# Two fused transformer blocks on one core: the level masks of the RWKV inverse made by GpSimd in place of VectorE

## The chip, the core and the metric
One NeuronCore of a Trainium2 chip runs the whole program, one launch for one sequence of 512 tokens. The metric is the device time of that launch in microseconds (us), lower is better. Engines are named as in the profile: PE (TensorE matmul), PEld (its weight load), DVE (VectorE), ACT (ScalarE), POOL (GpSimd), SP (SyncE, here only the queue that loads weights).

## What is computed
The reference runs two transformer blocks on x of 512 x 1024, float32. The first mixes a dilated window attention with an RWKV-7 layer, gates and merges both, projects, and adds a squared-ReLU feed-forward. The second mixes a pooling branch with a windowed attention and ends in a gated feed-forward. The change lies in the RWKV-7 layer, whose recurrence, cut to what matters, is for each of 16 heads of width 64:

```
def step(state, inp):
    r_t, w_t, k_t, v_t, kk_t, a_t = inp
    sa = einsum('bhij,bhj->bhi', state, -kk_t)
    state = state * w_t + sa * (kk_t * a_t) + v_t * k_t
    y_t = einsum('bhij,bhj->bhi', state, r_t)
    return state, y_t
```

The kernel computes it in four chunks of 128 tokens. Within a chunk the 128 dependent values of sa are found at once: with a strictly triangular matrix A (the gram of the decayed keys against each other), sa comes out of the inverse of a unit triangular matrix made of A. That inverse is built by doubling: blocks of 2, 4, 8, up to 128 tokens, seven levels. At each level the part of A that links the two halves of each block is taken out by multiplying A with a 0/1 mask of that level, and two rounds of matmuls bring the inverse from one block size to the next.

## The kernel before
**Weights.** Every product with a weight is made of three float32r matmuls (high times high, high times low, low times high; lines 572 to 574 of the trace). Weights come in units of 128 x 2048 into a ring of three slots. SP loads a unit (w_raw), ACT copies its high part (w_hi, line 1215), and the low part w_lo = w_raw - w_hi is written over w_raw. POOL does this in a loop over all 138 units (line 563), except for the units from DVE_LO0 to DVE_LO1 - 1, which belong to the RWKV stage: their low parts are made by DVE (weights_behind, line 1880).

**The RWKV stage.** Heads are handled in 8 pairs. For each pair the arrays are 128 x 512 (128 partitions, 4 chunks of 128), and there is one of each per head of the pair (index h = 0, 1). The stage is a software pipeline over steps p from -2 to 7: in step p, pair a = p is in its last phase (the recurrence over chunks, the norm), pair b = p + 1 is in the inverse, pair c = p + 2 is in its first phase (decay, keys, bonus). Every engine has its own written-out order of the parts of a step, and all waits are on counting semaphores. PE also has slots in each step that it fills with pieces of the projections of later pairs (side_half, three 512-column matmuls each): these are the matmuls of lines 572 to 574 in this stage. Such a half can begin only when the half before has been taken out of its PSUM bank (shift_half on DVE, lines 1816 and 1817, whose other input gate_tile comes from ACT, line 1309).

**The inverse of pair b, engine by engine.** PE makes the gram (inverse_grams, line 944). DVE copies its strict triangle of both heads into GA, named gram_inv (line 1963), and then makes level 0's masked gram Mb, named level (line 1957), one instruction per head. PE turns it (level_x, line 956, level 0). DVE's level_first then makes TT = Mb + I (line 1970, named tinv_t) and Tb = x + I (line 1972, named tinv) for each head, and after both makes the masks of level 1. From level 1 on: PE's level_x multiplies Mb with Tb (line 956), DVE adds the identity (level_x, line 1979, named xinv), PE's level_t makes both products (lines 964 and 966), ACT copies them back to TT and Tb (lines 1431 and 1432). At the end a refinement (lines 973, 1984, 980, 1989) gives the inverse that pair a's recurrence uses (line 1004). The masks of levels 2 to 6 stand at places of their own in DVE's step, each right before or some operations before the next level's matmuls need them. There is one Mb per head, so a mask can be written only once the matmuls of the level before have read the last one.

**The start of a step** is a chain through engines: PE's bonus sum (line 915), DVE's bonus (1947), tinv_full (1989) and kb (1952, 1953), PE's gram (944), DVE's gram_inv (1963), the masks of level 0 (1957), PE's level_x (956). Meanwhile PE has the sigmoid inputs of pair c (882) and the first solve of pair a (1004) to do.

Of the kernel before, what the change touches and what calls it, by code (L numbers as in the profile page):

```python
# [12 lines left out]
ALU = mybir.AluOpType  # L13
AX = mybir.AxisListType

P = 128
T = 512
NT = T // P
# [17 lines left out]
PAIRS = 8  # L36
# [5 lines left out]
LEVELS = (2, 4, 8, 16, 32, 64, 128)  # L42
# [91 lines left out]
CC = {}  # L134
# [64 lines left out]
def build(nc, x, wpack, lora_wa, lora_g, params, rel_bias, post_gains, sink, ctab, btab, icount, out):  # L199
# [7 lines left out]
    with ExitStack() as ctx:  # L207
# [9 lines left out]
        def fixed(name, shape, dt=F32):  # L217
            return place(name, shape, dt)[0]
# [12 lines left out]
        def sem(name):  # L231
            return ctx.enter_context(nc.semaphore(name))
# [13 lines left out]
        C = fixed("consts", [P, N_EARLY_CCOLS])  # L246
# [61 lines left out]
        GA = [r(f"gram_inv{h}", [P, NT, P]) for h in range(2)]  # L308
        Mb = [r(f"level{h}", [P, NT, P], F32R) for h in range(2)]
# [79 lines left out]
        rs = {n: sem(n) for n in (  # L389
            "z_full", "sig_ready", "zg_full", "g_ready", "sq_ready", "ss_full", "nrm_ready", "rn_ready", "rnx_ready", "rb_full",  # L390
            "kk_ready", "rk_ready", "bonus_full", "bon_ready", "csm_ready", "exps_ready", "xexp_ready", "ra_ready",
            "kb1_ready", "kb_ready", "tok_full", "tok_ready", "agram_full", "gram_full", "gram_taken", "m_ready",
            "x_full", "x1_ready", "tt_full", "t_ready", "t2_ready", "s_ready", "rhs_full", "rhs_ready", "sa_full",
            "sa_ready", "s_full", "y_full", "yraw_ready", "mu_full", "ysq_ready", "var_full", "std_ready",
            "rv_ready", "rvx_ready", "rvb_full", "rvm_ready", "u_full", "e_ready", "c_full", "tf_ready")}

# [33 lines left out]
        DVE_LO0, DVE_LO1 = UNIT0["gate1_first"], UNIT0["rwkvb"] + 1  # L430
# [35 lines left out]
        def f32(ap):  # L466
            return ap.bitcast(F32)
# [14 lines left out]
        for hp in range(2):  # L482
            for qt in range(NT):
                mats, vals, off = [], [[], []], 0
                for g in range(N_GROUPS):
                    nb = min(2, qt + 1) if g == 0 else qt + 1
                    k0 = (qt + 1 - nb) * P
                    for e in range(2):
                        h = g * 4 + 2 * hp + e
                        rows = slice(HD * e, HD * e + HD)  # L490
                        b, c0 = (3 + 2 * g - 2 + e, 0) if g else (2, 256 * e)
# [16 lines left out]
        for j in range(Q_HEADS2 // 2):  # L508
            for qt in range(NT):
# [4 lines left out]
                n = (hi - lo) * P  # L514
                pairs2.append(dict(
                    n=n, j=j, rows=rows, bias=AD[:, x0:x0 + n], out=O2[:, j, qt * P:(qt + 1) * P],
# [37 lines left out]
        @block.gpsimd  # L554
        def _(pool):


            for n in range(N_UNITS):
                if DVE_LO0 <= n < DVE_LO1:
                    continue  # L560
                slot = n % RING
                pool.wait_ge(hi_ready, n + 1)
                nc.gpsimd.tensor_tensor(Wl[:, slot, :], raw[:, slot, :], f32(Wh[:, slot, :]),  # L563
                                        ALU.subtract).then_inc(lo_ready, 1)
# [1170 lines left out]
        def _(dve):  # L1735
            order = Order(dve, dve_order)
            v = nc.vector
# [89 lines left out]
            for i, it in enumerate(pairs1):  # L1827
                st, n = 16 + 8 * (i % 2), it["n"]
# [4 lines left out]
                for m in it["mats"]:  # L1833
                    ins = v.scalar_tensor_tensor(LG[:, m["e"], m["off"]:m["off"] + m["n"]], m["dst"], HD ** -0.5, m["bias"],
                                                 ALU.mult, ALU.add)
# [20 lines left out]
            def cast4(ap):  # L1856

                return ap.unsqueeze(1).to_broadcast([P, NT, P])

            nl = len(LEVELS)  # L1860
# [3 lines left out]
            def lmask(lv):  # L1864
                return cast4(C[:, CC["levels"] + lv * P:CC["levels"] + (lv + 1) * P])

            def w(name, per, pair, k):
                dve.wait_ge(rs[name], per * pair + k)

            def inc(ins, name):  # L1870
                ins.then_inc(rs[name], 1)
# [15 lines left out]
            def shift_half(n):  # L1887
                if n is not None and HALVES[n][0] == "rkv":
                    kind, pair, part = HALVES[n]
                    shift(N_SHIFTED[n], RKV[:, pair % 2, part, :], 0, GT, 8 * part + pair)  # L1890
# [61 lines left out]
                inc(v.tensor_tensor(KB[:, 1, :], Ab[:], X2[:], ALU.mult), "kb1_ready")  # L1952
                inc(v.tensor_tensor(KB[:, 0, :], kk_, X2[:], ALU.mult), "kb_ready")

            def level_mask(b, lv):
                for h in range(2):
                    inc(v.tensor_tensor(Mb[h][:], GA[h][:], lmask(lv), ALU.mult), "m_ready")  # L1957

            def inverse_grams(b):
                w("agram_full", 1, b, 1)  # L1960
                v.memset(stat[:, 40:41], 0.0)
                for h in range(2):
                    ins = v.copy_predicated(GA[h][:], mask[:, P:2 * P].unsqueeze(1).to_broadcast([P, NT, P]), b3(4 + h))
                order(ins)
                level_mask(b, 0)

            def level_first(b):
                for h in range(2):
                    w("m_ready", 2 * nl, b, h + 1)
                    v.tensor_tensor(TT[h][:], f32(Mb[h][:]), cast4(ident), ALU.add)  # L1970
                    w("x_full", 2 * nl, b, h + 1)
                    inc(v.tensor_tensor(Tb[h][:], b3(4 + h), cast4(ident), ALU.add), "t2_ready")
                w("t2_ready", 2, b, 2)
                level_mask(b, 1)

            def level_x(b, lv):
                for h in range(2):
# [13 lines left out]
            def solved(a, t):  # L1991
                w("sa_full", NT, a, t + 1)
                inc(v.tensor_copy(SA[:], ps[:, 3, P:2 * P]), "sa_ready")
# [37 lines left out]
            def step(p):  # L2031

                a, b, c = p, p + 1, p + 2
                has_a, has_b, has_c = 0 <= a, 0 <= b < PAIRS, c < PAIRS
                first, middle, _ = STEP_HALVES[p]
                last = STEP_HALVES[p - 1][2] if p > -2 else None
                if has_b:
                    inverse_grams(b)
                shift_half(last)
                if has_a:  # L2040
                    solved(a, 0)
                if has_b:
                    level_first(b)
                if has_a:
                    state(a, 0)
                weights_behind(last)
                if has_c:
                    key_squares(c)
                if has_b:
                    level_x(b, 1)  # L2050
                if has_a:
                    solved(a, 1)
                if has_b:
                    level_mask(b, 2)
                if has_a:
                    state(a, 1)
                if has_c:
                    decay_sums(c)
                    key_scale(c)
                if has_b:  # L2060
                    level_x(b, 2)
                if has_a:
                    solved(a, 2)
                if has_b:
                    level_mask(b, 3)
                if has_a:
                    state(a, 2)
                shift_half(first)
                if has_c:
                    key_root(c)  # L2070
                if has_b:
                    level_x(b, 3)
                if has_a:
                    solved(a, 3)
                if has_c:
                    bonus_terms(c)
                    decay_args(c)
                if has_b:
                    level_mask(b, 4)
                if has_c:  # L2080
                    key_norm(c)
                    rates(c)
                weights_behind(first)
                if has_b:
                    level_x(b, 4)
                if has_a:
                    centred(a)
                if has_b:
                    level_mask(b, 5)
                    level_x(b, 5)  # L2090
                if has_c:
                    queries(c)
                if has_b:
                    level_mask(b, 6)
                shift_half(middle)
                if has_b:
                    grams(b, 0)
                if has_a:
                    norm_root(a)
                if has_b:  # L2100
                    level_x(b, 6)
                    grams(b, 1)
                weights_behind(middle, 0)
                if has_a:
                    normed(a)
                if has_b:
                    grams(b, 2)
                weights_behind(middle, 1)
                if has_b:
                    refine_e(b)  # L2110
                    grams(b, 3)
                if has_c:
                    bonus(c)
                if has_b:
                    refine_t(b)
                if has_c:
                    keys(c)
# [94 lines left out]
            for i, it in enumerate(pairs2):  # L2212
                st, n = 16 + 8 * (i % 2), it["n"]
# [4 lines left out]
                for h in range(2):  # L2218
                    ins = v.scalar_tensor_tensor(LG[:, h, 1:n + 1], it["bias"], it["slopes"][h], bank(4 + h, n),
                                                 ALU.mult, ALU.add)  # L2220
# [28 lines left out]
            for g in range(FF2_GROUPS):  # L2249
                d = USE0["ffn2"] + 2 * g  # L2250
                dve.wait_ge(hid_raw, FF1_GROUPS + g + 1)
                h = HID[:, 2 * g:2 * g + 2, :]
# [91 lines left out]
```

## Time and profile before

| | us |
|---|---|
| median of 3 runs | 1986.84 (1982.43 to 1988.65) |
| the profiled execution, its own time | 1984.22 |
| its span in the profile | 1982.4 |
| PE busy | 1875.3 (95%) |
| DVE busy | 881.5 (44%) |
| ACT busy | 760.0 (38%) |
| POOL busy | 514.0 (26%) |

The stage that the change touches runs from about 313 us (the first mask) to about 813 us. In it DVE is busy for three quarters of the time and POOL not at all. The page is an average over stages with different limits, so the busy shares above say little of this stage; it has to be read from windows of its own.

### The profile page before, as it was taken

Reading aid. Unit: us, or ns where it says so; the run is one execution under the profiler, and the core shown is the slowest. Engines: PE = TensorE matmul, PEld = TensorE weight load, DVE = VectorE, ACT = ScalarE, POOL = GpSimd, SP = SyncE. Lnnn points to the kernel's source line nnn. Section 1 sums busy time; section 2 is a strip of 40 time slices with the busy share of each in tenths; the row PEclk is TensorE's granted clock in tenths of the full one; section 3 lists DMA queues with packets and bytes.
Section 4 is the critical chain, followed back from the end, with each engine's and each line's share of the span. In section 5 each row is a group of like instructions: output and inputs, shape, how many; then the busy total and the mean of one; then the engine's idle time right before and its main releaser. Section 6 shows DMA issues by size and latency. Waiting matters only on the chain.

```text
span 1982.4 us, 23689 instructions
## 1 busy us (share of the span) xinstructions
PE 1875.3 (95%) x10148; PEld 1549.8 (78%) x10148; DVE 881.5 (44%) x1321; ACT 760.0 (38%) x1099; POOL 514.0 (26%) x115
## 2 busy tenths in 40 slices
PE   6999878999999999899899999989999999999998
PEld 5887656878878888688788888877776788888886
DVE  2015436687778776443301344351774341013333
ACT  5226534445544553423422222252564242222222
POOL 2431200000000000034243444423223424343432
PEclk8999988899999999999999999999999999999999
DMA  4711122000100000243223232322112223232221
GB/s 152 249 65 64 59 70 61 25 25 22 44 27 25 22 22 32 89 150 113 105 97 103 89 106 85 106 89 91 64 64 85 85 96 106 86 106 90 101 101 70
DMA packets 54508, 160.74 MB, mean 81 GB/s; under 512 B 3295, under 2 KB 30303, under 8 KB 39684
## 3 DMA queue, kind: packets, MB, share of 16 engines
q1 hardware_dynamic: 42476, 135.40, 19.8%
q10 hardware_dynamic: 11928, 23.83, 3.5%
q8 instruction: 80, 1.31, 0.3%
q14 instruction: 24, 0.20, 0.0%
HBM read 152.63 MB, written 10.25 MB: 82 GB/s over the span
## 4 chain that ended last, share of the span: by engine, by line
PE 83%; ACT 7%; DVE 7%; issue 1%; DMA 1%; POOL 0%; ACTq 0%; DVEq 0%
PE ps L572 23%; PE ps L573 22%; PE ps L574 22%; PE ps L956 2%; PE ps L966 2%; PE ps L964 2%; ACT w_hi L1215 1%; PE ps L1040 1%; PE ps L688 1%; ACT tinv_t L1431 1%; PE ps L1004 1%; PE ps L973 1%; DVE level L1957 1%; DVE x_res L1768 1%; PE ps L666 1%
## 5 line engine op out<-in xcount | busy, mean ns | idle before, releaser
L563 POOL TENSOR_TENSOR w_lo<-w_raw,w_hi 128x2048 fp32r<-128x2048 f32 x111 | 513.8, 4629 | 1438.3 <-ACT w_hi L1215 1438.3
L572 PE MATMUL ps<-ht_hi,w_hi 128*128 128x512 f32 (+1 forms) x1304 | 529.3, 406 | 22.3 <-DVE ht_lo L1754 9.9
L574 PE MATMUL ps<-ht_hi,w_lo 128*128 128x512 f32 (+1 forms) x1304 | 502.3, 385 | 0.0
L573 PE MATMUL ps<-ht_lo,w_hi 128*128 128x512 f32 (+1 forms) x1304 | 502.3, 385 | 0.0
L1215 ACT ACTIVATE w_hi<-w_raw 128x2048 fp32r<-128x2048 f32 x126 | 240.9, 1914 | 489.0 <-PE ps L574 430.6
L572 PEld LDWEIGHTS ps<-ht_hi,w_hi 128*128 128x128 f32 x1304 | 250.8, 192 | 84.5 <-issue 32.7
L574 PEld LDWEIGHTS ps<-ht_hi,w_lo 128*128 128x128 f32 x1304 | 250.4, 192 | 49.3
L573 PEld LDWEIGHTS ps<-ht_lo,w_hi 128*128 128x128 f32 x1304 | 251.3, 193 | 39.5 <-issue 2.2
L2161 DVE TENSOR_TENSOR hid_lo<-hidden,hid_hi 128x1024 fp32r<-128x1024 f32 x27 | 129.3, 4788 | 149.1 <-ACT hid_hi L1580 149.1
L572 PE MATMUL ps<-w_hi,hid_hi 128*128 128x512 f32 x432 | 168.1, 389 | 0.0
L574 PE MATMUL ps<-w_hi,hid_lo 128*128 128x512 f32 x432 | 168.1, 389 | 0.0
L573 PE MATMUL ps<-w_lo,hid_hi 128*128 128x512 f32 x432 | 168.1, 389 | 0.0
L574 PEld LDWEIGHTS ps<-w_hi,hid_lo 128*128 128x128 f32 x432 | 81.1, 188 | 16.9
L572 PEld LDWEIGHTS ps<-w_hi,hid_hi 128*128 128x128 f32 x432 | 81.1, 188 | 16.8
L573 PEld LDWEIGHTS ps<-w_lo,hid_hi 128*128 128x128 f32 x432 | 81.1, 188 | 16.7
L572 PE MATMUL ps<-w_hi,ht_hi 128*128 128x512 f32 (+2 forms) x256 | 86.6, 338 | 2.1 <-POOL w_lo L563 2.1
L1431 ACT ACTIVATE tinv_t<-ps 128x512 fp32r<-128x512 f32 x96 | 57.7, 601 | 78.2 <-PE ps L966 78.2
L573 PE MATMUL ps<-w_lo,ht_hi 128*128 128x512 f32 (+2 forms) x256 | 86.5, 338 | 0.0
L574 PE MATMUL ps<-w_hi,ht_lo 128*128 128x512 f32 (+2 forms) x256 | 86.5, 338 | 0.0
L2170 DVE TENSOR_TENSOR hidden<-ps,gate_act 128x1024 f32<-128x1024 f32 x16 | 19.6, 1225 | 134.1 <-ACT gate_act L1619 134.1
L1957 DVE TENSOR_TENSOR level<-gram_inv,consts 128x512 fp32r<-128x512 f32 x112 | 72.1, 685 | 0.6
L1979 DVE TENSOR_TENSOR xinv<-ps,consts 128x512 fp32r<-128x512 f32 x96 | 61.3, 678 | 19.0 <-PE ps L956 18.8
(290 smaller groups left out, 2595.9 us busy)
## 6 DMA issues: line engine op xcount, KB each, us to landing
w_raw<-in_wpack SPq DMA_DIRECT2D x114, 1024.0 KB, 4.8
w_raw<-in_wpack SPq DMA_DIRECT2D x24, 512.0 KB, 5.2
bias_skewed_dram<-bias_rows_dram ACTq DMA_DIRECT2D x1, 3840.0 KB, 22.9
toe<-bias_skewed_dram ACTq DMA_DIRECT2D x1, 3072.0 KB, 13.2
x_res<-in_x SPq DMA_DIRECT2D x4, 512.0 KB, 5.6
merged<-gate_dram ACTq DMA_DIRECT2D x1, 2048.0 KB, 11.1
gate<-gate_dram ACTq DMA_DIRECT2D x1, 2048.0 KB, 13.3
x_res<-in_x ACTq DMA_DIRECT2D x1, 2048.0 KB, 8.8
```

Of the source, the lines that this page charges most:

```text
L563: nc.gpsimd.tensor_tensor(Wl[:, slot, :], raw[:, slot, :], f32(Wh[:, slot, :]), ALU.subtract).then_inc(lo_ready, 1)
L572: mm(dst, wh, ah, start=first, stop=False)
L573: mm(dst, wh, al, start=False, stop=False)
L574: return mm(dst, wl, ah, start=False, stop=last)
L956: last = mm(ps[:, 4 + h, tok(t)], Mb[h][:, t, :], Tb[h][:, t, :] if lv else identR[:], start=True, stop=True)
L964: mm(ps[:, 6 + h, tok(t)], Xb[h][:, t, :], TT[h][:, t, :], start=True, stop=True)
L966: last = mm(ps[:, 4 + h, tok(t)], TT[h][:, t, :], Xb[h][:, t, :], start=True, stop=True)
L1215: actf(Wh[:, n % RING, :], raw[:, n % RING, :], ACT.Copy).then_inc(hi_ready, 1)
L1431: actf(TT[h][:].rearrange("p a b -> p (a b)"), bank(6 + h), ACT.Copy)
L1957: inc(v.tensor_tensor(Mb[h][:], GA[h][:], lmask(lv), ALU.mult), "m_ready")
L1979: inc(v.tensor_tensor(Xb[h][:], b3(4 + h), cast4(ident), ALU.add), "x1_ready")
L2161: v.tensor_tensor(HIl[:, 2 * g:2 * g + 2, :], HID[:, 2 * g:2 * g + 2, :], f32(HIh[:, g % RING, :, :]), ALU.subtract).then_inc(hid_lo, 1)
```

## The change
The 112 mask instructions (8 pairs, 7 levels, 2 heads) leave DVE and are issued by POOL. POOL does them in one block of its program, between the low part of the last unit before the RWKV stage and that of the first unit after DVE's own. DVE's copy of the gram now signals ga_ready in place of the wait that ordered it before the masks. POOL waits for ga_ready at level 0 and, at level 1, for t2_ready of the same head (DVE has then read Mb for TT). For every mask but the first two it also waits for x_full of the level before and the same head, so that PE has read Mb. Nothing is changed in PE's and ACT's programs, nor in DVE's except for the masks, the order wait and DVE's own wait on t2_ready. The instruction is the same in shape: 128 x 512, the gram times a mask of 128 columns repeated over the four chunks.

```diff
         @block.gpsimd
         def _(pool):
+            nl = len(LEVELS)
+
+            def level_mask(b, lv, h):
+
+                if lv == 0:
+                    pool.wait_ge(rs["ga_ready"], b + 1)
+                if lv == 1:
+                    pool.wait_ge(rs["t2_ready"], 2 * b + h + 1)
+                if b or lv:
+                    pool.wait_ge(rs["x_full"], 2 * (nl * b + lv - 1) + h + 1)
+                cols = C[:, CC["levels"] + lv * P:CC["levels"] + (lv + 1) * P].unsqueeze(1).to_broadcast([P, NT, P])
+                nc.gpsimd.tensor_tensor(Mb[h][:], GA[h][:], cols, ALU.mult).then_inc(rs["m_ready"], 1)
+
             for n in range(N_UNITS):
                 if DVE_LO0 <= n < DVE_LO1:
+                    if n == DVE_LO0:
+                        for b in range(PAIRS):
+                            for lv in range(nl):
+                                for h in range(2):
+                                    level_mask(b, lv, h)
                     continue
...
-            def level_mask(b, lv):
-                for h in range(2):
-                    inc(v.tensor_tensor(Mb[h][:], GA[h][:], lmask(lv), ALU.mult), "m_ready")
-
             def inverse_grams(b):
...
-                order(ins)
-                level_mask(b, 0)
+                inc(ins, "ga_ready")
 
             def level_first(b):
...
                     inc(v.tensor_tensor(Tb[h][:], b3(4 + h), cast4(ident), ALU.add), "t2_ready")
-                w("t2_ready", 2, b, 2)
-                level_mask(b, 1)
...
-                if has_b:
-                    level_mask(b, 2)
```

The calls for levels 3 to 6 leave DVE's step in the same way.

## Rows read from the trace of the kernel before

**Rows 1.** The page: busy time, and the chain that ended last, by engine.
```profile
PE 1875.3 (95%) x10148; PEld 1549.8 (78%) x10148; DVE 881.5 (44%) x1321; ACT 760.0 (38%) x1099; POOL 514.0 (26%) x115
...
PE 83%; ACT 7%; DVE 7%; issue 1%; DMA 1%; POOL 0%; ACTq 0%; DVEq 0%
```

**Rows 2.** Windows, step p = 1, and the sum of all eight: each engine's busy us.
```profile
435.40:498.20 62.80, 61.04 (x431) 51.02 (x431) 48.45 (x93) 31.51 (x52) 0.00 (x0) 1.00 0.08 21
...
sum 499.40, PE 476.87 PEld 402.89 DVE 372.40 ACT 243.25 POOL 0.00; mean PE 59.61 PEld 50.36 DVE 46.55 ACT 30.41 POOL 0.00
```

**Rows 3.** Waits of PE, 300 to 810 us: total us, times, longest.
```profile
PE ps L964 <- DVE xinv L1979: 5.0, 3, 3.2
...
PE ps L572 <- DVE rkv L1817: 4.8, 12, 0.6
PE ps L956 <- DVE level L1957: 3.9, 5, 1.3
PE ps L944 <- DVE kb L1952: 2.6, 2, 1.3
```

**Rows 4.** Groups of DVE by form, 300 to 810 us: masks and DVE's own low parts.
```profile
L1957 DVE TENSOR_TENSOR level<-gram_inv,consts 128x512 fp32r<-128x512 f32 x112 | 72.1, 685 | 0.6
...
L1880 DVE TENSOR_TENSOR w_lo<-w_raw,w_hi 128x2048 fp32r<-128x2048 f32 x8 | 18.3, 2285 | 0.1
```

**Rows 5.** Groups and waits of POOL over the whole span.
```profile
L563 POOL TENSOR_TENSOR w_lo<-w_raw,w_hi 128x2048 fp32r<-128x2048 f32 x111 | 513.8, 4629 | 1438.3 <-ACT w_hi L1215 1438.3
L2334 POOL MEMSET const-bfloat16-1.0<- 128x1 bf16 x1 | 0.1, 102 | 0.0
...
POOL w_lo L563 <- ACT w_hi L1215: 1438.3, 109, 594.6
```

**Rows 6.** Timelines of POOL and DVE at one hid_lo (start, us); DVE's group.
```profile
1100.49 4.61 POOL L563 TENSOR_TENSOR w_lo<-w_raw,w_hi 128x2048 fp32r<-128x2048 f32 x1 [6.28 <-ACT w_hi L1215]
...
1101.39 4.79 DVE L2161 TENSOR_TENSOR hid_lo<-hidden,hid_hi 128x1024 fp32r<-128x1024 f32 x1 [1.52 <-ACT hid_hi L1580]
...
L1880 DVE TENSOR_TENSOR w_lo<-w_raw,w_hi 128x1024 fp32r<-128x1024 f32 x8 | 9.6, 1213 | 3.5 <-ACT w_hi L1215 3.5
```

**Rows 7.** Timeline of DVE at the start of step p = 1.
```profile
436.07 0.71 DVE L1963 COPY_PREDICATED gram_inv<-consts,ps 128x512 f32<-128x512 int32 x1
436.82 1.29 DVE L1957 TENSOR_TENSOR level<-gram_inv,consts 128x512 fp32r<-128x512 f32 x2
438.03 0.74 DVE L1816 SCALAR_TENSOR_TENSOR rkv<-ps,one_less_mu,gate_tile 128x511 f32<-128x511 f32 x1
...
439.14 0.68 DVE L1970 TENSOR_TENSOR tinv_t<-level,consts 128x512 fp32r<-128x512 f32 x1
...
441.66 1.29 DVE L1957 TENSOR_TENSOR level<-gram_inv,consts 128x512 fp32r<-128x512 f32 x2
```

**Rows 8.** Timeline of PE in the same stretch.
```profile
437.57 1.26 PE L956 MATMUL ps<-ident_r,level 128*128 128x128 f32 x8 [0.73 <-DVE level L1957]
...
442.40 1.26 PE L956 MATMUL ps<-tinv,level 128*128 128x128 f32 x8
```

**Rows 9.** Step p = -1: DVE's low part behind the masks, and PE's wait for xinv.
```profile
318.52 2.29 DVE L1880 TENSOR_TENSOR w_lo<-w_raw,w_hi 128x2048 fp32r<-128x2048 f32 x1
...
322.58 0.66 PE L964 MATMUL ps<-tinv_t,xinv 128*128 128x128 f32 x4 [1.47 <-DVE xinv L1979]
```

**Rows 10.** Later in step p = 1: DVE's xinv of levels 4 and 5, and PE.
```profile
470.05 1.28 DVE L1979 TENSOR_TENSOR xinv<-ps,consts 128x512 fp32r<-128x512 f32 x2
...
474.96 1.29 DVE L1979 TENSOR_TENSOR xinv<-ps,consts 128x512 fp32r<-128x512 f32 x2 [0.93 <-PE ps L956]
...
480.32 0.50 PE L572 MATMUL ps<-ht_hi,w_hi 128*128 128x512 f32 x1 [0.31 <-DVE rkv L1817]
```

**Rows 11.** Windows at the starts of steps p = 1 and p = 2, with PE's granted clock.
```profile
436.00:442.30 6.30, 5.45 (x34) 4.12 (x33) 6.20 (x13) 1.97 (x2) 0.00 (x0) 1.00 0.00 0
499.00:505.30 6.30, 5.40 (x29) 4.24 (x28) 6.20 (x12) 2.42 (x4) 0.00 (x0) 0.73 0.31 130
```

More of the change, by code:

```diff
@@ L392, in build @@
             "kb1_ready", "kb_ready", "tok_full", "tok_ready", "agram_full", "gram_full", "gram_taken", "m_ready",
-            "x_full", "x1_ready", "tt_full", "t_ready", "t2_ready", "s_ready", "rhs_full", "rhs_ready", "sa_full",
+            "ga_ready", "x_full", "x1_ready", "tt_full", "t_ready", "t2_ready", "s_ready", "rhs_full", "rhs_ready", "sa_full",
             "sa_ready", "s_full", "y_full", "yraw_ready", "mu_full", "ysq_ready", "var_full", "std_ready",
@@ L2063, in step @@
                     solved(a, 2)
-                if has_b:
-                    level_mask(b, 3)
                 if has_a:
@@ L2077, in step @@
                     decay_args(c)
-                if has_b:
-                    level_mask(b, 4)
                 if has_c:
@@ L2088, in step @@
                 if has_b:
-                    level_mask(b, 5)
                     level_x(b, 5)
@@ L2092, in step @@
                     queries(c)
-                if has_b:
-                    level_mask(b, 6)
                 shift_half(middle)
```

## The prediction
> **What bounds the kernel now.** The page first: PE is busy for 95% of the span, and the chain that ended last runs through PE for 83% of it and through DVE for 7% [rows 1]. That says only that PE is the engine to watch. The change touches one stage, so the second view is windows cut at the starts of the steps. A full step takes 63 us and PE is busy for 61 of them; over the eight steps it is busy for 476.9 of 499.4 us [rows 2]. DVE, with 48 of 63 us, is well used but not the bound, and POOL does nothing. So 22.5 us of PE's idle time is all that shorter queues can win back, unless PE's clock also changes. The third view, PE's waits, shows which part of the idle time is DVE's: xinv 5.0, rkv 4.8, the masks themselves 3.9, kb 2.6, together 16.3 us [rows 3]. The question is which of these shrink and which grow.
>
> **The price of one mask.** On DVE it takes 685 ns, and 112 of them are 72.1 us of DVE's busy time, 9 us of each step [rows 4]. The trace has no POOL instruction of this size. Its only worker takes 4629 ns for 2048 columns, and its smallest instruction 102 ns [rows 5]. Below: all of it in proportion, 4629 / 4 = 1157 ns. Above: if POOL's time per column were no more than DVE's, (2285 - 1213) / 1024 = 1.05 ns [rows 4, 6], the fixed part would be 4629 - 2144 = 2485 ns and a mask would take 3.0 us. I take 1.2 us, next to the lower end, because a fixed part of over 2 us does not go with an instruction of 102 ns. The two heads' masks follow each other, 2.4 us, where DVE needs 1.29.
>
> What the pages would make of it: the Trainium skill (GPSIMD Engine Reference, 3.1 Elementwise) measures such an operation at 1.96 times VectorE's time. By that a mask is 1.34 us (an estimate from that page), 0.14 more than I take, and with two masks at eight step starts the sum would be 2.2 us higher. No row shows this size.
>
> **POOL and DVE in each other's way.** DVE's hid_lo, 128 x 1024 with both inputs in SBUF, starts 0.90 us after a POOL low part has started and takes 4.79 us; the same kind and size takes 1.21 us while POOL rests. POOL ends at 1105.10 and hid_lo at 1106.18, 1.08 us behind [rows 6]. So DVE did not run slower, it stood until POOL was through. Taking this as it reads, a DVE instruction with two inputs in SBUF stands up to 1.2 us behind a POOL mask, and one whose other input is in PSUM (xinv, rkv, tinv) is taken as free. The Trainium skill has this as a rule (SBUF — State Buffer, Who interferes with whom): such a VectorE instruction and a GpSimd one that reads SBUF exclude each other for their whole length, whichever comes first. By that rule POOL can also stand behind DVE; the trace agrees for DVE behind POOL, with the 4.79 us. Without any such exclusion the first-step term below (+1.7) would fall away.
>
> **Part 1: level 0, at the start of each step.** Before: DVE's second gram_inv ends at 436.78, the masks run from 436.82 to 438.11, PE's level_x starts at 437.57 after an idle 0.73, does head 0 and head 1 without a break and ends at 438.83 [rows 7, 8]. After: POOL starts at about 436.86, head 0 is ready at 438.06 and head 1 at 439.26. PE starts at 438.1 (0.6 later), stands again between the heads, and ends head 1 at 439.26 + 0.6 = 439.9, 1.1 us later than before. What hides it? Nothing: PE takes its work in order, and the side matmul behind it waits. DVE's rkv shift comes 1.2 us earlier, since the masks no longer stand before it, but it only removes a wait that would have been over anyway. PE's end of level 0 thus moves by 1.1 us in each of eight steps: **+8.8 us**. It is +8.0 at 1157 ns and some +37 at 3.0 us (3.6 later for head 1, plus the 1.1).
>
> **Part 2: level 1.** DVE's level_first now waits in DVE's queue for m_ready from POOL. Behind it stand pair a's state, the low part w_lo, pair c's key squares and xinv. TT of head 0 reads Mb and the identity, both in SBUF, so it stands until head 1's mask ends at 439.26, where it started at 439.14 before [rows 7]. Hardly later, then. Its four operations end at about 441.7 as before. POOL's masks of level 1 start behind TT of head 1 (440.5 to 441.1): head 0 at 442.3, head 1 at 443.5. Before, they were there at 442.34 and 442.95. PE comes to level_x of level 1 at 442.40 [rows 8], now at 443.5: on time. So **0** in a full step, between 0 and +0.6 (if PE comes no later than before). In the first step PE has no pair a to work on. Head 1's mask of level 1 would end near 320.2, and w_lo (2.29 us, two SBUF inputs) starts behind it, where it started at 318.52; xinv and PE's level_t, which already waited 1.47 us [rows 9], follow 1.7 us later: **+1.7**. If w_lo gets in first, the mask comes 2.3 us later still; that is the upper end, +4.
>
> **Part 3: levels 2 to 6.** POOL may start a mask as soon as PE's level_x of the level before is done; PE needs it one xinv, eight matmul groups and two ACT copies later, 4.9 us at the least in step p = 1, from xinv of level 4 to xinv of level 5 [rows 10]. Two masks take 2.4. They are off the path, at 0, and held behind a w_lo of 2.29 us they would still be there in time, at 4.7. DVE loses ten masks at 0.6 us of spacing, but it does not get all of it: the masks now run right beside xinv, and the next DVE operation with two SBUF inputs (decay sums, bonus terms, squares, queries) stands for up to 1.1 us behind the second. Some half comes through. The PE wait it can shorten is that of 0.31 us for the rkv shift that stands behind level 6's masks [rows 10]; the rest of the rkv waits hang on ACT's gate_tile. 0.31 us in six full steps: **-1.9 us**. Ends: 0, and -12.4, which is all of the waits for xinv, rkv and kb in rows 3.
>
> **Part 4: PE's clock.** At the start of step p = 2 the granted clock is 0.73 in a window of 6.3 us, so PE spent part of it at 1.2 in place of 2.4 GHz; at the start of step p = 1, with the same busy time, it stayed at 1.00 [rows 11]. Both had short stops just before. Cost of one such drop: 0.27 x 6.3 = 1.7 us. The same windows at the seven starts from p = 0 on show a drop at five (0.52 to 0.88) and none at p = 1 and 4. With a stop that grows from 0.7 to over 1.3 us, and a second between the heads, one of these two falls, I take it: **+1.7 us**, between 0 and +7 (both, and longer ones elsewhere).
>
> **Part 5: POOL's queue.** The masks stand before the low part of the first unit behind the stage. POOL's longest wait is 594.6 us [rows 5]; that gap holds the stage, so 112 x 1.2 = 134 us fit in. DVE's last mask ended near 795 us, the stage near 813. No DMA is issued by POOL or DVE, and SP's loads wait for PE alone. **0.** If the cover were gone, a low part would come one mask late, 1.2 us, once.
>
> **Sum:** 8.8 + 0 + 1.7 - 1.9 + 1.7 + 0 = +10.3 us. On the profiled execution's own 1984.22 us this is 1994.5. That execution is 2.6 us below the median shown, 1986.84; a median of new runs should stand by the median, so the forecast is **1997 us**, 0.52% above. About 0.3% (6 us) is what a measurement of this kernel can tell from no change.
>
> **The rivals.**
> - *The delay is absorbed* (0.26). The 1.1 us at level 0 is partly paid by time that PE would idle later in the step (1.8 us per full step, rows 2), and DVE's lighter queue takes more of it away. For: the rkv waits, 12 of them. Against: what PE waits for later was itself started by PE, and moves with it. Half of part 1 gone and the clock unchanged: 4.4 + 1.7 - 1.9 = +4.2, 1991 us.
> - *Faster* (0.12). The mechanism is DVE's queue: with 9 us less in each step every DVE result comes before PE asks. The waits for xinv, rkv and kb go (-12.4), and four of the five step starts with a clock drop keep the full clock (-1.7 each, -7). Level 0 costs 8.8 as above. Net -10.6: 1976 us. It decides where DVE's delay, and not PE's or ACT's own work, is what starts a step; against it speaks that PE had to wait for kb, DVE's last work of a step, only twice [rows 3].
> - *The exclusion makes masks late everywhere* (0.10). DVE has long two-input operations between levels; if POOL loses its turn to them at each level, PE waits 0.6 us at levels 1 to 6 in eight steps, 29 us, and the sum is +39: 2026 us; half of the levels give 2011. Against it: the 4.9 us between levels.
> - *The change does not do what it says* is no case here: m_ready is only counted by POOL's masks.
>
> **How the numbers follow.** The forecast has 0.52, with its own range +6 to +17, 1993 to 2004 (parts 2 and 4 at their ends, a mask of 1.3 us). The range runs from 1985 to 2010: it leaves out most of the faster case and the far half of the late-mask case. Faster by over 0.3%: 0.12. Within: the absorbed case and the forecast's low edge, 0.28. Slower: 0.60.
>
> **What would show it.** POOL would show 112 masks of 1.15 to 1.35 us in the stage. DVE's busy time there falls by less than 72 us, because tinv_t, scans, kb or squares that stand behind POOL are shown longer than 0.7 us. PE's wait for level at level 0 would rise from 3.9 us to about 12, and a full step from 63 to 64 us. More windows at step starts would show a clock under 1. The forecast is wrong if the step stays at 63 us or less, if PE's waits for level don't grow, or if they appear at levels 2 to 6 too.

## The result and the profile after

The changed kernel takes 2005.37 us in the median of 4 runs (2003.70 to 2006.06) against 1987.31 us before: a ratio of 1.0094, 95% interval 1.0076 to 1.0112, so 18 us or 0.9% slower. The forecast was slower, 1997 us, with 1985 to 2010 as the range. The profiled execution has a span of 2003.4 us, 21.0 more than that of the kernel before.

The page of the changed kernel, the lines that answer to [rows 1] and the new group on POOL:

```profile
PE 1892.7 (94%) x10148; PEld 1564.1 (78%) x10148; DVE 834.7 (42%) x1209; ACT 760.3 (38%) x1099; POOL 643.8 (32%) x227
...
PE 81%; issue 6%; ACT 6%; DVE 5%; POOL 1%; DMA 1%; ACTq 0%; DVEq 0%; POOLq 0%
...
L569 POOL TENSOR_TENSOR level<-gram_inv,consts 128x512 fp32r<-128x512 f32 x112 | 130.1, 1182 | 418.0 <-DVE gram_inv L1977 206.4
```

DVE lost 72.1 us of masks but is only 46.8 us less busy: 25 us came back as other instructions that are shown longer. PE has the same 10148 matmuls and is 17.4 us longer busy with them. That is work at a lower clock (windows below), and it is the first hint that PE's standing is only part of the loss.

PE's waits in the changed kernel, from 300 to 840 us, to be read against [rows 3] (L974 is level_x, L982 level_t, L590 the side matmul):

```profile
PE ps L974 <- POOL level L569: 11.2, 13, 2.4
...
PE ps L982 <- DVE xinv L1990: 5.4, 7, 3.3
PE ps L962 <- DVE kb L1970: 2.6, 2, 1.3
PE ps L590 <- DVE rkv L1835: 2.6, 5, 0.6
```

The wait for the masks grew from 3.9 to 11.2 us, that for rkv fell from 4.8 to 2.6. Windows cut at the first gram copy of each step tell what each cost. First the kernel before, steps p = -1, 0 and 5, then the changed one; PE's busy time is the fourth number, the granted clock the third from the end:

```profile
312.20:369.90 57.70, 49.59 (x309) 42.16 (x308) 40.06 (x75) 26.55 (x44) 0.00 (x0) 0.90 0.14 44
369.90:435.40 65.50, 64.53 (x431) 53.77 (x431) 50.38 (x95) 31.07 (x52) 0.00 (x0) 0.93 0.07 19
...
690.00:753.50 63.50, 59.73 (x406) 50.34 (x404) 47.69 (x91) 30.17 (x50) 0.00 (x0) 0.92 0.06 17
```

```profile
312.50:377.00 64.50, 54.95 (x309) 46.34 (x309) 34.69 (x59) 26.69 (x44) 18.45 (x14) 0.81 0.13 39
377.00:443.50 66.50, 65.32 (x431) 54.03 (x431) 44.17 (x82) 31.07 (x52) 15.55 (x14) 0.93 0.07 19
443.50:508.20 64.70, 62.18 (x431) 52.12 (x430) 43.01 (x79) 31.52 (x52) 15.84 (x14) 0.97 0.08 22
...
703.90:771.70 67.80, 62.84 (x406) 53.27 (x404) 41.94 (x77) 30.28 (x50) 16.99 (x14) 0.87 0.06 16
```

Two sums over the seven steps from p = -1 to p = 5 divide the loss. **Idle** is length less PE's busy time. **Clock loss** is (1 - granted clock) x length. The seven steps took 441.3 us before and 459.2 after, 17.9 more. Idle went from 20.4 to 26.2, clock loss from 19.3 to 33.6. Length is idle plus busy time, so of the 17.9 us, 5.8 are PE standing, a third, and 12.1 are PE busy for longer with the same matmuls. The clock loss tells why: it grew by 14.3, PE working at 1.2 in place of 2.4 GHz for a while after it stood. (It is not the 12.1 exactly, since it also counts the slow clock while PE stands, and the clock is given with two digits: 0.01 of a step is 0.6 us.) The first step alone grew by 6.8 us, of which 1.4 are idle, and p = 5 by 4.3. The other 3.1 of the 21.0 us between the two profiles lie behind the stage.

The timelines at the start of step p = 1 show a hand-over. First POOL, then DVE and PE:

```profile
444.89 2.14 POOL L569 TENSOR_TENSOR level<-gram_inv,consts 128x512 fp32r<-128x512 f32 x2 [23.07 <-DVE gram_inv L1977]
448.26 2.52 POOL L569 TENSOR_TENSOR level<-gram_inv,consts 128x512 fp32r<-128x512 f32 x2 [1.23 <-DVE tinv L1985]
```

```profile
446.02 1.56 DVE L1983 TENSOR_TENSOR tinv_t<-level,consts 128x512 fp32r<-128x512 f32 x1
...
446.04 0.66 PE L974 MATMUL ps<-ident_r,level 128*128 128x128 f32 x4 [1.17 <-POOL level L569]
447.09 0.66 PE L974 MATMUL ps<-ident_r,level 128*128 128x128 f32 x4 [0.39 <-POOL level L569]
...
448.01 0.63 PE L591 MATMUL ps<-ht_lo,w_hi 128*128 128x512 f32 x1
```

A mask takes 1.07 us. PE stands 1.17 and 0.39 us where it stood 0.73, and the 512-column matmul behind takes 0.63 us, not 0.40: the clock has fallen, in a step that kept it before [rows 11]. The matmul of the same place in the kernel before:

```profile
439.29 0.40 PE L573 MATMUL ps<-ht_lo,w_hi 128*128 128x512 f32 x1
```

DVE's tinv_t needs 1.56 us for 0.68 because it stands until POOL's second mask ends at 447.03.

### The profile page after: what moved, and what is told of

It reads as the page before. It is cut to its first block, busy times and chain, and to the rows that moved or that the text cites. A ratio compares the mean times of both kernels' runs of the same rounds, so it can differ in the third digit from the quotient of the medians.

```text
span 2003.4 us, 23719 instructions
## 1 busy us (share of the span) xinstructions
PE 1892.7 (94%) x10148; PEld 1564.1 (78%) x10148; DVE 834.7 (42%) x1209; ACT 760.3 (38%) x1099; POOL 643.8 (32%) x227
## 4 chain that ended last, share of the span: by engine, by line
PE 81%; issue 6%; ACT 6%; DVE 5%; POOL 1%; DMA 1%; ACTq 0%; DVEq 0%; POOLq 0%
PE ps L590 22%; PE ps L592 21%; PE ps L591 21%; PE ps L982 2%; PE ps L974 2%; PE ps L984 2%; ACT w_hi L1233 1%; POOL level L569 1%; PE ps L706 1%; PE ps L900 1%; DVE x_res L1786 1%; PE ps L684 1%; PE ps L1048 1%; PE ps L1022 1%; PE ps L727 1%
## 5 line engine op out<-in xcount | busy, mean ns | idle before, releaser
L590 PE MATMUL ps<-ht_hi,w_hi 128*128 128x512 f32 (+1 forms) x1304 | 531.9, 408 | 18.0 <-DVE ht_lo L1772 9.0
L590 PEld LDWEIGHTS ps<-ht_hi,w_hi 128*128 128x128 f32 x1304 | 252.4, 194 | 80.0 <-issue 30.2
L569 POOL TENSOR_TENSOR level<-gram_inv,consts 128x512 fp32r<-128x512 f32 x112 | 130.1, 1182 | 418.0 <-DVE gram_inv L1977 206.4
L590 PE MATMUL ps<-w_hi,hid_hi 128*128 128x512 f32 x432 | 168.1, 389 | 0.0
L590 PEld LDWEIGHTS ps<-w_hi,hid_hi 128*128 128x128 f32 x432 | 81.1, 188 | 16.9
L1449 ACT ACTIVATE tinv_t<-ps 128x512 fp32r<-128x512 f32 x96 | 57.7, 601 | 83.0 <-PE ps L984 83.0
L590 PE MATMUL ps<-w_hi,ht_hi 128*128 128x512 f32 (+2 forms) x256 | 86.6, 338 | 2.1 <-POOL w_lo L581 2.1
```

The costliest lines, as they stand in the source:

```text
L569: nc.gpsimd.tensor_tensor(Mb[h][:], GA[h][:], cols, ALU.mult).then_inc(rs["m_ready"], 1)
L590: mm(dst, wh, ah, start=first, stop=False)
L1449: actf(TT[h][:].rearrange("p a b -> p (a b)"), bank(6 + h), ACT.Copy)
```

## The experiments

All of them are variations of the two kernels, each timed beside the kernel before on the same chip. Two theories stood at first. A: the loss comes from the hand-overs at levels 0 and 1. B: it comes from POOL and DVE excluding each other in the upper levels.

**Which levels.** A function decides who makes a mask, and each engine has a counter of its own:

```diff
+def on_pool(b, lv):
+    return lv >= 2                           # e1_high_pool
+    return lv < 2                            # e2_low_pool
+    return not (b == 0 and lv == 1)          # e3_first_dve
```

e1_high_pool. 

> Levels 2 to 6 on POOL, levels 0 and 1 back on DVE. Theory A (the loss comes from the two hand-overs to POOL at the start of each step: PE stands 1 us longer there, and its clock falls behind that): nearly all of the +18 us goes, 1984 to 1992 us; PE's idle time in the stage within 2 us of before (23.1). Theory B (POOL and DVE exclude each other, and DVE's long two-input operations stand behind the masks of levels 2 to 6): half or more of the loss stays, 1996 us or more.

Measured: 1998.1 us, ratio 1.0061 (1.0043 to 1.0080).

e2_low_pool. 

> Levels 0 and 1 on POOL, levels 2 to 6 back on DVE. Theory A: the loss is as in the full change or larger, because DVE has its 10 masks back: 2003 to 2010 us. Theory B: less than half of it, 1989 to 1996 us.

Measured: 1997.5 us, ratio 1.0060 (1.0040 to 1.0081).

Neither theory stands alone. Each half costs about 12 us by itself, and together they cost 18, so the two are not simply added. The trace of e1_high_pool shows what the upper levels do, in step p = 2. DVE, POOL, PE:

```profile
512.76 2.28 DVE L1914 TENSOR_TENSOR w_lo<-w_raw,w_hi 128x2048 fp32r<-128x2048 f32 x1
514.96 1.32 DVE L1928 TENSOR_SCALAR kk<-rkv,params_sb 128x512 f32<-128x512 f32 x1
516.31 1.46 DVE L1929 TENSOR_TENSOR work_x<-kk 128x512 f32<-128x512 f32 x1
517.70 1.27 DVE L2019 TENSOR_TENSOR xinv<-ps,consts 128x512 fp32r<-128x512 f32 x2
```

```profile
512.78 4.44 POOL L583 TENSOR_TENSOR level<-gram_inv,consts 128x512 fp32r<-128x512 f32 x2 [28.41 <-PE ps L990]
...
518.43 0.66 PE L998 MATMUL ps<-tinv_t,xinv 128*128 128x128 f32 x4 [1.84 <-DVE xinv L2019]
```

The masks of level 2 are released as soon as PE's level_x of level 1 is done, while DVE has the low part and the key squares ahead of xinv. POOL's first mask stands behind w_lo, then kk stands behind that mask (1.32 for 0.48), then work_x behind the second (1.46 for 0.69). xinv comes 1.6 us later, and PE stands 1.84 us for it. Nobody needed those masks yet. They were not late but early. In the first step the same thing makes PE stand 3.07 us for xinv, where it stood 1.47.

e3_first_dve. 

> The full change, but the two masks of level 1 of pair 0 are made by DVE, so that they no longer stand behind DVE's low part. Theory A with the sizes of the trace: the first step loses its wait of 2.44 us and the slow clock behind it, and becomes 4 to 5 us shorter: 2000 to 2002 us. If the first step's 6.8 us come from somewhere else (the clock alone, or xinv), 2004 to 2006 us.

Measured: 1999.5 us, ratio 1.0069 (1.0047 to 1.0090). The first step fell from 64.5 to 61.6 us, by 2.9 and not by 4 to 5, and the wait of 2.44 for the mask is gone; PE now stands 3.08 us for xinv there, behind level 2's early masks. All seven steps together are as long as in the change (458.9 and 459.2 us), because p = 4 and 5 are longer in this profile, and the intervals of the two ratios overlap. That the whole kernel gained by this edit is not shown.

**The clock.** In e4_filler PE works while it waits, in f1_before_filler too, with (2, 0) in place of (4, 1):

```diff
             def level_x(b, lv):
                 for h in range(2):
+                    if lv == 0:
+                        for _ in range((4, 1)[h]):
+                            mm(bank(6), identR[:], HTh[:, 0, :], start=True, stop=True)
```

e4_filler. 

> The full change, with PE made to work while it waits at level 0: four spare 512-column matmuls ahead of head 0's wait and one ahead of head 1's, results unused. If the clock is most of the loss (14 of 21 us by the windows), the drops at the step starts go and the time falls to 1991 to 1997 us, with a granted clock near 1 at the step starts. If the drops come anyhow, or the standing itself is the loss, 2003 to 2010 us.

Measured: 1999.1 us, ratio 1.0074 (1.0055 to 1.0093), less gain than expected. The interval overlaps with that of the full change (1.0076 to 1.0112), so the times alone don't show a gain. The windows are plainer. Step p = 1, changed kernel and then e4_filler:

```profile
444.00:450.30 6.30, 4.74 (x24) 3.75 (x25) 5.56 (x11) 1.97 (x2) 4.18 (x4) 0.79 0.00 1
```

```profile
444.60:450.90 6.30, 6.01 (x37) 4.39 (x37) 6.11 (x12) 1.97 (x2) 4.16 (x4) 1.00 0.00 1
```

The clock stays at 1.00, and over the seven steps the clock loss falls from 33.6 to 15.9 us and the steps by 10 us. With the same masks, the same hand-overs and only the standing filled, the drop does not come: the standing is what brings it. It does not bring it each time: in step p = 3 of e2_low_pool PE stands the same 1.17 and 0.39 us, and the clock of the step is 1.00.

f1_before_filler. 

> The kernel before, with two spare 512-column matmuls of PE ahead of head 0's wait at level 0 (results unused). In the kernel before, the windows put 22.8 us of lost time in the stage on the clock, part of it behind the starts of steps. If PE's stops at level 0 bring those drops, they go: 1976 to 1983 us, clock loss down by 4 to 10 us. If other stops bring them (ACT's rhs, kb), no change: 1984 to 1992 us.

Measured: 1984.5 us, ratio 0.9993 (0.9982 to 1.0004): no difference. In the profile the seven steps fell by 2.7 us, clock loss from 19.3 to 13.5, which the whole time does not show.

**POOL beside DVE, and nothing else.** f2_extra_pool is the kernel before, with POOL instructions whose result nobody uses (the spare row is written again later, and ACT waits for the last of them before that):

```diff
+            def extra_mask(b, lv, h):
+                pool.wait_ge(rs["x_full"], 2 * (nl * b + lv - 1) + h + 1)
...
+                nc.gpsimd.tensor_tensor(spare, cols, cols, ALU.mult).then_inc(rs["extra_made"], 1)
```

> The kernel before with all its own masks on DVE, and beside them 80 POOL instructions of a mask's size (levels 2 to 6, both inputs from SBUF, result unused), each released when the change would release it. Nothing waits for them on the path. If POOL and DVE exclude each other and this is what costs in the upper levels, the time rises by 8 us or more, 1994 to 2005 us, with xinv waits of PE in the steps whose low part stands before xinv. If the exclusion is harmless, 1984 to 1990 us.

Measured: 1995.9 us, ratio 1.0047 (1.0026 to 1.0068). 80 instructions that no engine waits for on the path cost 9 us; PE's waits for xinv rose from 5.0 to 12.0:

```profile
PE ps L979 <- DVE xinv L1996: 12.0, 10, 3.3
```

The profiled execution, 2003.7 us in span, was the longest of its five, so only the ratio is read as the cost. All masks that are used are DVE's here, as before, so neither a late mask nor a hand-over can be the reason: POOL's work beside DVE's costs time by itself, as theory B says.

**A later start.** The masks of levels 2 to 6 wait for DVE's xinv as well:

```diff
+                if lv > 1:
+                    pool.wait_ge(rs["x1_ready"], 2 * (nl - 1) * b + 2 * (lv - 2) + h + 1)
```

f3_high_late (levels 2 to 6). 

> Levels 2 to 6 on POOL as in e1_high_pool, but each mask also waits until DVE's xinv of the level before and the same head is done. Then no mask can stand in front of the operations that DVE has to get through before xinv. If the early start of the masks is the cause in e1_high_pool (waits of 3.07 and 1.84 us for xinv), they shrink to those of before and the time is 1983 to 1990 us. If the masks come too late now, PE waits for level at levels 2 to 6: 1993 us or more.

Measured: 1987.0 us, ratio 0.9994 (0.9982 to 1.0007). One wait more on POOL takes away all of the 12 us of e1_high_pool. In the first step xinv again starts behind operations of their usual length; the scan behind it pays now (2.80 for 1.36), where nobody waits:

```profile
320.66 0.69 DVE L1931 TENSOR_TENSOR work_x<-kk 128x512 f32<-128x512 f32 x1
321.27 1.28 DVE L2021 TENSOR_TENSOR xinv<-ps,consts 128x512 fp32r<-128x512 f32 x2
322.47 2.80 DVE L1936 TENSOR_TENSOR_SCAN cum_decay<-consts,sig_w 128x128 f32<-128x128 f32 x4
...
322.11 2.25 POOL L585 TENSOR_TENSOR level<-gram_inv,consts 128x512 fp32r<-128x512 f32 x2 [59.15 <-DVE xinv L2021]
```

f4_all_late (all levels). 

> The full change with the same later start of the masks of levels 2 to 6. What is left is the hand-over at levels 0 and 1: 1995 to 2000 us, as in e2_low_pool. If the two parts are not separate, 2002 us or more.

Measured: 1994.8 us, ratio 1.0047 (1.0030 to 1.0064). The full change with this wait loses half as much; the rest goes with levels 0 and 1. Of the 11.0 us between the spans of the two profiles, 5.1 lie in the seven steps, so how the gain comes about is seen only in part.

**Together.** g1 is f3 with f1's filler; g2 has more filler in pair 0's level_t, 3 matmuls at level 1 and 7 at level 3; g3 and g4 put the low levels back on POOL.

g1_high_late_filler. 

> Levels 2 to 6 on POOL with the later start (as f3_high_late), and the two spare matmuls of f1_before_filler at level 0. If what DVE gains in room and what the filler saves of the clock (5.8 us by the windows of f1_before_filler) add up, 1980 to 1984 us, clear of before. If PE's own work is the bound and both only shift its stops, 1984 to 1989 us.

Measured: 1984.2 us, ratio 0.9991 (0.9982 to 1.0000). Hardly more than nothing.

g2_more_filler. 

> The same, and in the first step of the inverse also 3 and 7 spare matmuls ahead of PE's waits for xinv at levels 1 and 3 (1.47 and 3.25 us before). If the slow clock behind these two stops goes, 3 to 5 us below g1_high_late_filler. If the filler takes PE's time from real work, the same or slower than it.

Measured: 1980.2 us, ratio 0.9971 (0.9961 to 0.9981). It beats both kernels, by 0.3% and 1.2%. The first step takes 54.0 us for 57.7, at a clock of 0.99 for 0.90, though PE does ten matmuls more in it than in g1:

```profile
313.10:367.10 54.00, 48.27 (x321) 39.47 (x321) 37.31 (x63) 26.35 (x44) 11.27 (x10) 0.99 0.15 47
```

The gain over g1 is filler alone. The kernel before has the same two waits (1.47 and 3.25 us), so it might gain by the filler too; that was not tried. Nothing here shows that POOL's masks have a part in the gain.

g3_all_late_filler. 

> All masks on POOL except level 1 of pair 0, with the later start at levels 2 to 6 and the filler of e4_filler (4 and 1) at level 0. The three causes found so far (early masks of the upper levels, pair 0's level 1 behind the low part, the clock at the step starts) are then all treated, and what is left is the hand-over itself, some 1.0 us of PE standing or of filler at eight starts: 1987 to 1993 us. If something else is in the full change's loss, 1996 us or more.

Measured: 1996.3 us, ratio 1.0056 (1.0038 to 1.0074), above the 1987 to 1993 us expected: treating the three causes was not enough. Its seven steps take 445.5 us, 4.2 over before, where the time is 10 over. Inside, step p = 2 takes 69.6 us, with this stop and a slow clock behind it:

```profile
507.18 0.66 PE L995 MATMUL ps<-tinv,level 128*128 128x128 f32 x4 [1.35 <-POOL level L585]
```

The same stop in p = 0 and p = 4 (1.35 and 1.34 us) leaves the clock at 1.00.

g4_not_one. 

> As g3_all_late_filler, with level 1 of every pair on DVE (levels 0 and 2 to 6 on POOL, later start, filler 4 and 1 at level 0). In g3_all_late_filler PE still stood 1.35 us for level 1's mask in steps p = 2 and 4, where DVE's low part follows level_first, and its clock fell behind one of them. If level 1 is what was left, those waits go, steps 2 and 4 take 63 to 64 us, and the time is 1984 to 1989 us. If level 0's hand-over is what was left, 1991 us or more.

Measured: 1992.9 us, ratio 1.0046 (1.0029 to 1.0064). The stop at level 1 is gone and p = 2 and 4 take 63.3 us each, as the one theory had it, yet the time is on the other's side. What is left sits in two steps: the first (60.9 us, PE again waits 1.46 for xinv, clock loss 9.1) and p = 5 (67.0, a new wait of 1.22 for xinv, clock loss 6.7). In all other steps of this profile level 0 on POOL costs nothing once PE's standing is filled. The times say less: the ratio is 1.0046, and the profiled execution was the shortest of the five.

The seven steps in numbers, us, worked out from each profile as above:

| kernel | length | PE idle | clock loss | ratio of times |
|---|---|---|---|---|
| before | 441.3 | 20.4 | 19.3 | 1 |
| the change | 459.2 | 26.2 | 33.6 | 1.0094 |
| e1_high_pool | 452.3 | 25.9 | 24.3 | 1.0061 |
| e2_low_pool | 451.7 | 26.5 | 25.7 | 1.0060 |
| e3_first_dve | 458.9 | 29.4 | 27.5 | 1.0069 |
| e4_filler | 449.1 | 21.7 | 15.9 | 1.0074 |
| f1_before_filler | 438.7 | 18.3 | 13.5 | 0.9993 |
| f2_extra_pool (longest of its runs) | 462.2 | 27.1 | 35.0 | 1.0047 |
| f3_high_late | 442.0 | 19.5 | 20.7 | 0.9994 |
| f4_all_late | 454.1 | 25.6 | 29.5 | 1.0047 |
| g1_high_late_filler | 438.5 | 17.5 | 14.6 | 0.9991 |
| g2_more_filler | 434.6 | 15.7 | 8.8 | 0.9971 |
| g3_all_late_filler | 445.5 | 20.8 | 13.2 | 1.0056 |
| g4_not_one | 445.2 | 17.5 | 19.1 | 1.0046 |

A profile is one execution, and its clock drops differ from the next one's; the ratios are the verdict, the columns say where. What comes behind the stage took 1167 to 1176 us in these profiles, without an order that follows the edits, so a profile's span can't settle a difference of a few us. One thing stays open. The three kernels with level 0 on POOL and the filler of 4 and 1 (e4, g3, g4) lose 9 to 15 us by their ratios, 5 to 7 us more than their seven steps show. So filling PE's standing did not win back the loss of the low levels in the whole time, and the runs don't show why.

Idle and clock loss also stand in for each other. In step p = 2 PE waits 1.38 us for a mask of level 1 in e2_low_pool, whose clock stays at 1.00, and not at all in the change. There PE works at the slow clock and comes to the matmuls of level 1 only 9.0 us behind the first gram copy, not 7.5, and by then both masks are made. The step takes 64.8 us in the one and 65.4 in the other. First e2_low_pool, then the change:

```profile
515.69 0.66 PE L990 MATMUL ps<-tinv,level 128*128 128x128 f32 x4 [1.38 <-POOL level L583]
```

```profile
517.22 1.00 PE L974 MATMUL ps<-tinv,level 128*128 128x128 f32 x8
```

## Why the prediction was right, and where its terms were not

**The price of a mask** was taken as 1.2 us with 1157 ns as the lower end. It is 1.07 (half of the 2.14 of two), below that end: a POOL instruction whose second input repeats 128 columns is not priced by the plain one in proportion. The estimate worked out from the Trainium skill (GPSIMD Engine Reference, 3.1 Elementwise), 1.34 us, is further off still: POOL's time is 1.56 times VectorE's 0.685 here, and not 1.96 times.

**Part 1, level 0: +8.8.** Right in kind, and too large. PE's head 1 ends 2.94 us behind the gram copies in step p = 1 (447.75 less 444.81) where it ended 2.05 behind them, so 0.9 us and not 1.1. In step p = 0 PE has no such wait, before or after. Over the stage PE's waits for level 0 rose from 3.5 to 8.8 us, by 5.3. All seven steps together gained 5.8 us of idle.

**Part 2, level 1: 0, and +1.7 in the first step with +4 as the upper end.** The upper end was the case. DVE's w_lo got its turn between POOL's two masks, the second came 2.44 us too late for PE, and the first step grew by 6.8 us with the clock. The full steps were taken at 0, and the change's own profile has no such stop in them. This is partly luck: with the clock at 1.00 a stop of 1.4 us for the second mask does appear where a low part stands in the same place (e2_low_pool in p = 2, g3 in p = 0, 2 and 4).

```profile
318.36 2.58 DVE L1898 TENSOR_TENSOR w_lo<-w_raw,w_hi 128x2048 fp32r<-128x2048 f32 x1
...
321.95 1.12 PE L974 MATMUL ps<-tinv,level 128*128 128x128 f32 x4 [2.44 <-POOL level L569]
```

**Part 3, levels 2 to 6: -1.9.** The reading of the waits was right for rkv (4.8 to 2.6 us). The step that failed is "they are off the path, at 0". It asked only whether a mask could come too late. It did not ask what the mask keeps DVE from while it is made too early, though the exclusion was read from [rows 6] two paragraphs before. It was assumed to fall behind xinv, and it falls ahead of it wherever DVE has something to do before xinv. By itself this part costs 12 us (e1_high_pool), and in the full change a later start takes back 9 us (f4_all_late); it is not a gain of 1.9. The change's own profile shows little of it as standing: PE's waits for xinv are 5.4 us for 5.0, with a stop of 0.36 us in each of six steps that had none. The rival "the exclusion makes masks late everywhere" had the resource right and the victim wrong for these levels: DVE's operations were late, not the masks.

**Part 4, the clock: +1.7, ends 0 and +7.** This term carried the loss and lay outside its own ends: 14.3 us of clock loss more over seven steps. Both starts that had kept the clock lost it, as one of the ends said, but the larger pieces were in the first step (+6.5), which the seven windows of the prediction left out, and in p = 5 (+3.7), where no new drop had been looked for because one was there already.

The trace shows a clock of 0.79 where PE stood for 1.56 us and 1.00 where spare matmuls filled most of that time. The Trainium skill (TensorE: Matmul & The Clock Gate, HAM oscillation — how this bites in real kernels) describes a kernel whose matmuls alternate with stops of PE and start at the slow clock behind each of them. The trace agrees in kind only: the stops of the page's example are longer ones, for DMAs, while here 1.17 and 0.39 us of waiting for another engine were enough in some steps and not in others.

**Part 5, POOL's queue: 0.** Nothing contradicts it: POOL's first low part behind the stage waits for ACT as before.

The sum, 10.3, against 18 measured: parts 1 and 2 were near, part 3 had the wrong sign, part 4 was eight times too small. That it came out slower rests on a mechanism that was read rightly, the hand-over at level 0 and the first step. That 2005 us lies inside the range is partly luck: it lies outside the forecast's own 1993 to 2004, and the terms that carried the loss, the clock and the early masks, were put at 1.7 and below nothing. The rivals of no change and of a gain are out by the interval. That DVE's lighter queue would pay is not borne out by f3 either: with 10 masks a step less on DVE, PE's waits for rkv fell from 4.8 to 3.0 us, and the time is the same as before within 0.2%.

## What to carry to other kernels

Work moved to GpSimd is not off VectorE's back: while it ran, VectorE's operations with all their inputs in SBUF stood. So it should be released as late as its reader allows and behind VectorE's urgent work, not as early as its inputs allow; here one added wait was worth 12 us (e1_high_pool to f3_high_late). And a stop of TensorE is to be priced with the slow clock that can follow it: the added stops were 6 us here, and the matmuls took 12 us longer. Where levels 0 and 1 lose in the whole time even with the stops filled is still open.

## What the runs showed that was not expected

- An operation of DVE with a single tensor input in SBUF stands behind POOL as well: kk, a tensor_scalar, took 1.32 us for 0.48 beside a mask, and its mean in the stage rose from 478 to 837 ns in e1_high_pool. The prediction had counted on two-input operations alone. xinv, with one input in PSUM and one in SBUF, kept its 678 ns on average.
- The turn changed at each instruction where both had work queued. In step p = 2 of e1_high_pool w_lo, mask, kk, mask, work_x went one after the other, each engine standing for the other in between. POOL's two masks then took 4.44 us for 2.14.
- Useless matmuls made a kernel faster: with 12 more of them in the first step (2 at level 0, 10 in level_t) it is 3.7 us shorter than before, and g2_more_filler, 10 matmuls more than g1_high_late_filler, is 4 us faster than it.
